# A third norm taken row by row inside the last feed-forward round, state-space tables made in that round, and three waits on weight rests moved

## What is computed

```python
# first block (end)
h = rms_norm(x, norm_ffn)
ff = square(relu(h @ w_ff1))          # 1024 -> 4096
x = x + ff @ w_ff2                    # 4096 -> 1024
x = rms_norm(x, norm_final)           # the "third norm"
# second block
u, h, c_gate, b_gate, gate_a, gate_b = split(x @ w_in_2 + b_in_2)
y_a = s5_ssm(u, ...)                  # 32 groups of 16 channels, 64 complex states each
#   dt = exp(log_dt); lb = exp(lambda * dt); powers of lb; (lb - 1) / lambda * b
y_a = gelu(y_a) * sigmoid(gelu(y_a) @ glu_w + glu_b) @ w_ssm_out
y_b = (b_gate * causal_conv(c_gate * h)) @ w_conv_out
merged = sigmoid(gate_a) * y_a + sigmoid(gate_b) * y_b
x = layer_norm(ALPHA * x + merged @ w_o)
x = layer_norm(ALPHA * x + (silu(x @ w_gate) * (x @ w_up)) @ w_down)
```

## Time and profile before

| | |
|---|---|
| median of 3 runs | 2930.26 us (2927.21 to 2930.47) |
| the profiled execution | 2929.72 us, its span 2927.8 us |
| TensorE (PE) busy | 2784.1 us, 95% of the span |
| VectorE (DVE) busy | 1293.1 us, 44% |
| ScalarE (ACT) busy | 710.6 us, 24% |
| GpSimd (POOL) busy | 288.1 us, 10% |
| mean granted TensorE clock | 0.979 |
| chain that ended last | PE 86%, DVE 9%, ACT 2%, issue 2%, DMA 1% |
| a 1 MB feed-forward slab, issue to landing | 5.4 us |

### The profile page before, as it was taken

The page is one execution under the profiler, slowest core; times in us unless marked ns, Lnnn a source line. Parts: engine busy times, 40 slices in busy tenths (PEclk is TensorE's granted clock), DMA queues, the critical chain, the costliest instruction groups (busy, mean ns, idle before and its releaser), DMA issues.

```text
span 2927.8 us, 34813 instructions
## 1 busy us (share of the span) xinstructions
PE 2784.1 (95%) x14570; PEld 2163.6 (74%) x14570; DVE 1293.1 (44%) x1909; ACT 710.6 (24%) x1172; POOL 288.1 (10%) x160
## 2 busy tenths in 40 slices
PE   5999997996999999999998999999999999999998
PEld 2445446884468888888877888877897888888877
DVE  1465695774243333333338433434264333333325
ACT  4224335321131112221131222222222111121112
POOL 0000143420000000000001121115400000000000
PEclk9999998996999999999999999999999999999999
DMA  4002004203011111111112222234312111112101
GB/s 152 29 30 87 29 18 155 86 33 137 0 65 44 43 57 54 47 43 45 56 39 86 66 73 87 71 120 148 137 38 79 43 43 43 43 44 71 43 15 72
DMA packets 161698, 188.17 MB, mean 64 GB/s; under 512 B 13488, under 2 KB 119216, under 8 KB 160944
## 3 DMA queue, kind: packets, MB, share of 16 engines
q1 hardware_dynamic: 161584, 186.54, 19.7%
HBM read 160.10 MB, written 25.23 MB: 63 GB/s over the span
## 4 chain that ended last, share of the span: by engine, by line
PE 86%; DVE 9%; ACT 2%; issue 2%; DMA 1%; POOL 0%; DVEq 0%; SPq 0%; ACTq 0%
PE ps L1209 65%; PE ps L907 6%; PE ps L1175 4%; DVE sb L2183 2%; PE ps L972 2%; DVE sb L2185 2%; PE ps L879 1%; PE ps L1079 1%; PE ps L1371 1%; PE ps L1121 1%; DVE sb L2258 1%; PE ps L1117 1%; PE ps L1093 1%; DVE sb L2431 1%; PE ps L915 1%
## 5 line engine op out<-in xcount | busy, mean ns | idle before, releaser
L1209 PE MATMUL ps<-H_hi,v_hi 128*128 128x512 f32 x704 | 274.9, 391 | 8.7 <-DVE v_lo L2729 5.6
L1209 PE MATMUL ps<-H_lo,v_hi 128*128 128x512 f32 x704 | 274.6, 390 | 0.0
L1209 PE MATMUL ps<-H_hi,v_lo 128*128 128x512 f32 x704 | 274.4, 390 | 0.0
L1209 PE MATMUL ps<-F_hi,w_hi 128*128 128x512 f32 x512 | 200.0, 391 | 3.4 <-DVE F_lo L2350 3.4
L1209 PE MATMUL ps<-F_lo,w_hi 128*128 128x512 f32 x512 | 199.9, 390 | 0.0
L1209 PE MATMUL ps<-F_hi,w_lo 128*128 128x512 f32 x512 | 199.7, 390 | 0.0
L1209 PE MATMUL ps<-w_hi,ff_hi 128*128 128x512 f32 x512 | 199.2, 389 | 0.0
L1209 PE MATMUL ps<-w_lo,ff_hi 128*128 128x512 f32 x512 | 199.2, 389 | 0.0
L1209 PE MATMUL ps<-w_hi,ff_lo 128*128 128x512 f32 x512 | 199.2, 389 | 0.0
L2760 DVE TENSOR_TENSOR hg<-hg,ps 128x512 f32<-128x512 f32 x44 | 30.3, 688 | 357.2 <-PE ps L1209 357.2
L1209 PE MATMUL ps<-H_hi,tw_hi 128*128 128x512 f32 x448 | 176.5, 394 | 8.6 <-DVE sb L2668 8.6
(11 more groups left out here) (335 smaller groups left out, 5272.6 us busy)
## 6 DMA issues: line engine op xcount, KB each, us to landing
wraw<-in_w_ff SPq DMA_DIRECT2D x32, 1024.0 KB, 5.4
traw<-in_w_in SPq DMA_DIRECT2D x28, 512.0 KB, 4.4
sb<-in_w_in SPq DMA_DIRECT2D x6, 2048.0 KB, 7.9
vraw<-in_w_gate SPq DMA_DIRECT2D x22, 512.0 KB, 5.1
vraw<-in_w_up SPq DMA_DIRECT2D x22, 512.0 KB, 6.2
vraw<-in_w_down SPq DMA_DIRECT2D x11, 1024.0 KB, 4.8
sb<-in_x SPq DMA_DIRECT2D x4, 2048.0 KB, 10.2
sb<-c_rows SPq DMA_DIRECT2D x16, 512.0 KB, 4.9
```

The costliest lines, as they stand in the source:

```text
L1209: mm = nc.tensor.matmul(out_ap, stationary(a, k), moving(c, k), start=(k == 0 and n == 0), stop=(k == kts - 1 and n == 2))
```

## The change

The third norm is taken row by row. The second half of the last round's down product gets its own order of groups, `last_order`, with the transposes of row t-2 behind row t and the input product's rows behind them. The input product takes a bank per half row, and U is drained in 16 parts. The tables' code moves unchanged into two functions, one called in k = 1 of the last round, one behind row 2 of its first half. Their loads (and those of three small tables) move in front of the feed-forward's rounds. The buffers of the third norm's results change place. Three waits on rests: the output product asks for 15 rests for rows 0 to 3 and for 16 from row 4; the first output weights are split after ft = 5 instead of 6; slab 0 of the last round of the second feed-forward is split after q = 1 of the round before instead of after q = 3.

```diff
+def last_order():
+    order = []
+    for t in range(NT):
+        order += [("w", t)] + [("t", t - 2, h) for h in range(2) if t > 1]
+    for t in range(0, 4, 2):
+        order += [("u", 0, t), ("u", 0, t + 1)] + [("t", 6 + t // 2, h) for h in range(2)]
+    order += [("u", 0, t) for t in range(4, NT)] + [("u", 1, t) for t in range(NT)]
+    return {key: n for n, key in enumerate(order)}
...
 @block.sync
...
             sp.dma_start(gain, A["norm_final"].partition_broadcast(P)).then_inc(gain_in, 16)
+            sp.dma_start(s_lr, A["lam_re"]).then_inc(ssm_in, 16)
+            sp.dma_start(s_li, A["lam_im"]).then_inc(ssm_in, 16)
...
+            sp.dma_start(taps2, A["conv_taps_2"].rearrange("p (t k) -> p t k", k=3)).then_inc(b2_in, 16)
             rounds(sp, FF_ROUNDS, ff_loads)
...
+            wait_drained(sp, last_ff, 7)
             sp.dma_start(u_row, ...).then_inc(u_row_in, 16)
             for j in range(NT):
                 sp.wait_ge(norm_rows, 16 + j + 1)
-                sp.dma_start(x_rows[j], xn[:, j, :]).then_inc(x_out, 16)
+                sp.dma_start(x_rows[j], xl[j]).then_inc(x_out, 16)
+            sp.wait_ge(x_out, 16 * NT)
+            wait_full(sp, *last_rows("t", NT - 1, 1))
+            sp.dma_start(d_row, A["ssm_d"].partition_broadcast(P)).then_inc(d_row_in, 16)
...
 @block.tensor
...
             def ff_round(i, last):
...
+                        if last and h == 1 and t > 1:
+                            pe.wait_ge(norm_rows, 2 * NT + t - 1)
+                            turn_row(last_rows, xl[t - 2], t - 2)
             rounds(pe, FF_ROUNDS, ff_round)
-            rows_to_features(G_NORM3, xn)
...
+            pe.wait_ge(u_lo, 1)
+            for t in range(NT):
+                if t in (2, 4):
+                    j = NT - 3 + t // 2
+                    pe.wait_ge(norm_rows, 2 * NT + j + 1)
+                    turn_row(last_rows, xl[j], j)
+                rows_ready(last_rows, [t])
+                input_rows(0, t)
+            pe.wait_ge(u_lo, 2)
+            for t in range(NT):
+                input_rows(1, t)
...
-            pe.wait_ge(m_lo, 16)
             for c in range(2):
                 pe.wait_ge(wo_lo, c + 1)
                 for t in range(NT):
+                    if c == 0 and t % 4 == 0:
+                        pe.wait_ge(m_lo, 15 + t // 4)
...
 @block.scalar
...
             def ff_round(i, last):
...
                     if h == 0:
                         round_slab(3, i)
+                        if last:
+                            act.wait_ge(ssm_angle, 1)
+                            nc.scalar.activation(s_sin, s_th, ACT.Sin)
+                            nc.scalar.activation(s_half, s_th, ACT.Sin, scale=0.5).then_inc(ssm_sin, 1)
...
+            round_input_weights(0)
+            act.wait_ge(w_lo, 4 * FF_ROUNDS)
+            for t in range(NT):
+                wait_drained(act, last_ff, 8 + t)
+                wait_drained(act, *last_rows("w", t))
+                nc.scalar.activation(xl[t], X[:, t, :], ACT.Square, accum_out=ssum[:, t:t + 1]).then_inc(norm_sums, 1)
+                root(1, t)
+                if t > 1:
+                    round_row(last_rows, t - 2, Hs[0])
+            for t in (NT - 2, NT - 1):
+                round_row(last_rows, t, Hs[0])
+            round_input_weights(1)
...
-                if ft == 6:
+                if ft == 5:
                     round_wo(0)
...
+                    if isinstance(i, int) and i == F2_ROUNDS - 2 and q == 1:
+                        wait_full(act, start, 3)
+                        round_slab2(0, i + 1)
...
 @block.gpsimd
...
-                if ft == 6:
+                if ft == 5:
                     rest_wo(0)
...
 @block.vector
...
             def ff_round(i, last):
...
                     if k in (1, 4):
                         rest_slab(1 + k // 4, i)
+                    if last and k == 1:
+                        state_rates()
-                for h in range(2):
+                for h in range(1 if last else 2):
                     for t in range(NT):
...
+                        if last and t == 2:
+                            state_powers()
             rounds(dve, FF_ROUNDS, ff_round)
...
+            for t in range(NT):
+                b = wait_full(dve, *last_rows("w", t))
+                xs = X[:, t, 512:1024]
+                V.tensor_tensor(xs, xs, ps[:, b, :], ALU.add).then_inc(drained[b], 1)
+                if t > 0:
+                    last_scaled(t - 1)
+                dve.wait_ge(norm_sums, 2 * NT + t + 1)
+                V.tensor_scalar(rs_arg[:, t:t + 1], ssum[:, t:t + 1], 1.0 / D, EPS, ALU.mult, ALU.add).then_inc(root_ask, 1)
+                if t > 1:
+                    rest_row(last_rows, t - 2, Hs[0], xrest, 1)
+            last_scaled(NT - 1)
+            rest_row(last_rows, NT - 2, Hs[0], xrest, 1)
+            dve.wait_ge(norm_rows, 3 * NT)
+            dve.wait_ge(u_row_in, 16)
+            input_drain(0, 0)
+            input_drain(0, 1)
+            rest_row(last_rows, NT - 1, Hs[0], xrest, 1)
+            input_drain(0, 2)
+            input_drain(0, 3)
             dve.wait_ge(x_out, 16 * NT)
...
             angles(0)
+            for t in range(4, NT):
+                input_drain(0, t)
             step_weights(0)
-            for j in range(NT):
-                b = wait_full(dve, G_U, j)
-                V.tensor_tensor(U[:, j, :], ps[:, b, :], u_row, add).then_inc(drained[b], 1)
+            for t in range(NT):
+                input_drain(1, t)
...
+                    if isinstance(i, int) and i == F2_ROUNDS - 2 and q == 1:
+                        rest_slab2(0, i + 1)
...
                 if isinstance(i, int) and i == F2_ROUNDS - 2:
-                    for q in range(2):
-                        rest_slab2(q, i + 1)
+                    rest_slab2(1, i + 1)
```

More of the change, by code:

```diff
@@ L331, in build @@
         xn = area(AT_WORK + 8192, NT, D)
+        xl = [area((AT_WORK + 8192, AT_WORK + 16384)[t // 4] + D * (t % 4), D) for t in range(NT)]
         BZ = area(AT_WORK, WT, SEQ)
-        U = area(AT_WORK + 4096, NT, W2)
+        U = area(AT_X + 4096, NT, W2)
         YA = area(AT_WORK + 4096, WT, SEQ)
-        U2 = area(AT_WORK + 4096, 4, D)
         M = area(AT_WORK + 8192, KT, SEQ)
@@ L1878, in f2_round @@
                 if not last:
-                    for q in range(2 if isinstance(i, int) and i == F2_ROUNDS - 2 else 3):
+                    for q in (1,) if isinstance(i, int) and i == F2_ROUNDS - 2 else range(3):
                         wait_full(act, start, (3, 7, 23)[q], **at)
@@ L2366, in rest_slab, with tt2, ts2, exp_to @@
                                 ).then_inc(w_lo, 1)
+            mul, add, sub = ALU.mult, ALU.add, ALU.subtract
+            def tt2(out, a, b, op):
+                then(V.tensor_tensor(out, a, b, op))
+            def ts2(out, a, x, op0, y=None, op1=None):
+                if op1 is None:
+                    then(V.tensor_scalar(out, a, x, None, op0))
+                else:
+                    then(V.tensor_scalar(out, a, x, y, op0, op1))
+            def exp_to(out, x):
+                ts2(s_k, x, 1.0 / float(np.log(2.0)), mul, -1e6, ALU.max)
+                ts2(s_k, s_k, ROUNDER, add)
+                ts2(s_k, s_k, ROUNDER, sub)
+                then(V.scalar_tensor_tensor(s_r, s_k, -LN2_HI, x, mul, add))
+                then(V.scalar_tensor_tensor(s_r, s_k, -LN2_LO, s_r, mul, add))
+                ts2(s_r, s_r, -1.0, ALU.max, 1.0, ALU.min)
+                ts2(s_e, s_r, 1.0 / 5040, mul, 1.0 / 720, add)
+                for c in (1.0 / 120, 1.0 / 24, 1.0 / 6, 0.5, 1.0, 1.0):
+                    tt2(s_e, s_e, s_r, mul)
+                    ts2(s_e, s_e, c, add)
+                ts2(s_k, s_k, -127.0, ALU.max, 128.0, ALU.min)
+                ts2(s_k, s_k, 127.0, add, 8388608.0, mul)
+                then(V.tensor_copy(s_t1.bitcast(mybir.dt.int32), s_k))
+                tt2(out, s_e, s_t1, mul)
@@ new lines, in reduce_angle, with power_rows @@
+            def reduce_angle(out, x, k, clamp_out=None):
+                ts2(k, x, 1.0 / TWO_PI, mul, ROUNDER, add)
+                ts2(k, k, ROUNDER, sub)
+                then(V.scalar_tensor_tensor(out, k, -TWO_PI_HI, x, mul, add))
+                then(V.scalar_tensor_tensor(out, k, -TWO_PI_LO, out, mul, add))
+                return V.tensor_scalar(out, out, PI_IN, -PI_IN, ALU.min, ALU.max)
+            def power_rows(first, count, by):
+                lo, hi = slice(1, 1 + count), slice(first, first + count)
+                xr = pw_re[:, by, :].unsqueeze(1).broadcast_to([P, count, 16])
+                xi = pw_im[:, by, :].unsqueeze(1).broadcast_to([P, count, 16])
+                n = count * 16
+                t0, t1 = (early[q][:, 0:n].rearrange("p (a b) -> p a b", b=16) for q in range(2))
+                tt2(t0, pw_re[:, lo, :], xr, mul)
+                tt2(t1, pw_im[:, lo, :], xi, mul)
+                tt2(pw_re[:, hi, :], t0, t1, sub)
```

(12 more changed lines are left out.)

246 lines of the change are left out of this document (88 added, 158 removed).

## The result

Six runs of the changed kernel have a median of **2902.82 us** (2900.0 to 2905.1), six of the kernel before 2928.99 us (2927.21 to 2934.91). The ratio is 0.9908, 95% interval 0.9895 to 0.9921: 26 us faster. The prediction was 2902, range 2895 to 2911.

What follows compares the result with a forecast made beforehand. TensorE, busy 95% of the span, bounds the kernel, so only its stops and restarts can be won. Gains 14.9 - 0.5 + 5.9 + 7.4 = 27.7 us, from 2929.7, gave 2902 us, range 2895 to 2911.

Steps and rivals of the forecast that it cites:

- first tile earlier: Third norm's tail: first state-space tile starts at 1590.8 instead of 1603.8, 13.0 us, less 0.5 for a clock fall.
- no restart there: At the first state-space tile: without the 8.6-us stop, no slow-clock restart behind it, 1.9 us gained.
- merge stage: Output product: waiting for 15 rests and splitting weights earlier removes a 4.2-us stop and 1.7 us of restart; bounds 3.3 and 5.9.
- last round: Second feed-forward's last round: the earlier split of slab 0 removes a 5.6-us stop and 1.8 us of restart.
- The rates: State rates at k=1 of the last round: 16.3 us of VectorE, hidden by k=6, costed at nothing.
- The powers: State powers behind row 2 of the last round's first half: 15.3 us without POOL beside them, bounds 15.0 and 19.5.
- the table load: Row 0 of the third norm: the load for the root, behind the new sine, lies beside the path.
- The bank was free: First state-space tile: its bank is free at 1579 to 1589, with 2 to 11 us to spare.
- The pace: Third norm, rows 1 to 5: VectorE paces at 4.87 us a row against TensorE's 3.6; bounds 3.6 and 5.6.
- Rows slower: Third norm: powers keep 19.5 us or the table load costs 4 us, and rows take 5.3; 2908 us, 17%.
- A seam that doesn't close: Merge stage or last weight rest: a wait behind eats one small move, 5.9 or 7.4 us back; 2908 us, 10%.
- Slower by the clock: Third norm's rows and input product: the clock falls at 1516 and stays at half, net 30 us slower; 2960 us, 3%.

Runs made afterwards that it cites:

- POOL in the powers: Changed kernel with the cast of the first input weights right behind the sines, so GpSimd's 4.6-us pass falls into VectorE's powers: 2907.41 us.
- the variants: Changed kernel with part of the powers moved into VectorE's idle time (2897.27 us), with VectorE's rests one row cycle later (2902.3 us), or with both (2895.71, again 2893.5 us).
- the kernels with single edits: Changed kernel with only the output product's wait back to 16 rests: 2910.77 us; with only the first output weights' split back behind the seventh tile: 2904.3 us.
- the kernel with only the split back: Changed kernel with the split of the first output weights back behind the seventh tile, the wait staying at 15 rests: 2904.3 us.

## Why the prediction was right, step by step

The time, 2902, lies 0.8 us from the median of the first six runs. With the nine later ones the changed kernel's median is 2904.7, because ten of 15 fell on the upper level; the profiled execution, against which the sum was made, was at 2900.7. The sum's terms, against what the traces give (all positions of after are 1.5 us early from the start):

| term | predicted | before to after | same falls of the clock on both sides |
|---|---|---|---|
| first tile earlier | 13.0 - 0.5 | 12.8 | 12.8 |
| no restart there | 1.9 | 1.9 | 1.9 |
| merge stage | 4.2 + 1.7 | 3.7 + 1.7 | 4.3 + 1.7 |
| last round | 5.6 + 1.8 | 6.1 | 7.4 |
| sum | 27.7 | 26.2 | 28.1 |
| not forecast: clock behind the GLU's stop (at 1965 before) | 0 | 1.3 | 0.7 |
| not forecast: clock behind the 3.07-us stop | 0 | in the 6.1 | -1.3 |
| not forecast: earlier by the last round, in the main the clock near the start | 0 | 1.5 | 1.5 |
| all | 27.7 | 29.0 | 29.0 |

The last column takes each term from profiles in which the same stops lowered the clock. G to Z is 391.0 where it fell at the GLU's stop and no restart stood at G (POOL in the powers), so 1.9 of the 3.2 us are the restart and 1.3 the GLU's fall. The profiles with that fall have a Z to W 0.6 shorter (87.1 against 87.7), which gives back 0.6 of the 1.3.

**The norm's seam.** The rates (1457.7 to 1473.6) were hidden, as said: they shift the rest behind k = 4 by 4.7 us from the span's start (6.2 with the 1.5), and by the eighth cast VectorE waits 3.9 us for ScalarE again. The powers took 15.2 us (15.3 said). Row 0 was scaled by 1517.98 where, less 1.5, 1518.1 was said; row 5 by 1540.74 (1540.6); the first tile started at 1589.54 (1589.3). One step inside was wrong without harm: the table load of 1.28 us was said to lie beside the path, and lies on it. ScalarE squares row 0, loads, and only then takes the root VectorE waits for:

```profile
1513.91 1.28 ACT L1499 ACT_TABLE_LOAD   x1
```

VectorE's reciprocal at 1515.51 stands behind it by 0.83 us. It was paid by the 4.87 us taken for row 0, a full cycle with two rests (1.29 us) and a wait of 0.74 in it that row 0 does not have; in their place stood the waits of 1.30 us for the square and 0.83 for the root. Two errors of some 2 us met, and that row 0 came out to 0.1 us is luck. The bank was free as said: the step weights ended at 1580.4, inside the 1579 to 1589 less 1.5.

**The pace.** From row 2 on rows came every 4.85 us with 0.74 of waiting, as taken from the earlier trace rows, and the variants show both the pace setter (VectorE) and the reserve (0.84 us a row). Row 2 took 5.4, which is the 0.5 charged for the clock. TensorE's short stops were 0.55, 1.0 and 1.0 us ahead of rows 3 to 5, where some 1.3 ahead of each row was said.

**The merge stage.** The 15th rest was said to be ready 1.0 us ahead of TensorE; it was 1.07. The split's 1 us and the count's 4.2 are what the kernels with single edits show.

**The last round.** The mechanism and the price hold (7.4 when it alone is undone). The two profiles give 6.1 because of another stop of this stage. Its first timeline row is of the kernel before, the second of the one after:

```profile
2202.96 0.47 PE L1209 MATMUL ps<-H_hi,v_hi 128*128 128x512 f32 x1 [3.07 <-DVE H_lo L2350]
```

```profile
2180.09 0.77 PE L1228 MATMUL ps<-H_hi,v_hi 128*128 128x512 f32 x1 [3.07 <-DVE H_lo L2373]
```

The same stop of 3.07 us, 16 us into the stage; the matmul behind it took 0.47 us at full clock before and 0.77 at half clock after. That cost after 1.3 us. (In the kernel with only the split back the clock did not fall there either, and its F to E is 733.2, the shortest of all.) The other way round at the GLU's stop of 2.9 us, the row of before first:

```profile
1966.00:1968.00 2.00, 2.00 (x4) 0.92 (x3) 0.00 (x0) 0.00 (x0) 0.00 (x0) 0.50 1.00 412
```

```profile
1950.00:1952.00 2.00, 2.00 (x6) 0.83 (x5) 0.00 (x0) 0.00 (x0) 0.00 (x0) 1.00 1.02 418
```

The edits touch neither stop, and near 60 us the same program was seen both with and without a fall; that these two were chance as well is argued, since no second profile of the kernel before was taken. **What the prediction lacked** is this: it took the 1.7 to 1.9 us behind a stop as fixed, and compared sums of one execution to tenths. The terms themselves come to 28.1 against 27.7; that the total came out near 2902 is partly luck, in which falls of the clock the profiled runs had (+0.7, -1.3, +1.5) and on which level the runs fell.

**The rivals.** Rows slower: its table load came true, its price did not. A seam that doesn't close: not seen; the 13th rest was pushed towards the 14th's time as feared (they start at 2057.6 and 2060.2, with 1.28 us of POOL idle between them), and the 15th was not late. Slower by the clock: the clock did fall at the predicted place, and was back 4 us later in a stretch of stop and go with transposes. The Trainium skill's rule that transposes do not count as busy (TensorE: Matmul & The Clock Gate) would have kept it low by that rival; this trace does not bear that out for transposes mixed with matmuls. But the prediction's ground against this rival, "in every restart it was back within 4 us", was a wrong reading. The trace of the kernel before has a stretch in which the transposes run alone, four at a time with stops between, and there the clock stayed low:

```profile
692.97 1.11 PE L879 MATMUL ps<-sb 128*128 128x128 f32 x4 [17.18 <-DVE sb L2341]
695.03 1.11 PE L879 MATMUL ps<-sb 128*128 128x128 f32 x4 [0.94 <-DVE sb L2341]
```

```profile
692.00:709.00 17.00, 8.92 (x32) 5.72 (x32) 14.78 (x23) 4.59 (x8) 0.00 (x0) 0.50 0.70 250
```

It came back only at 713, behind 3.6 us of matmuls. That stretch agrees with the Trainium skill's rule; whether the transposes or the stops kept the clock low there, no run separates. So the rival had a precedent in this very kernel, and its 3% rested on less than the prediction thought. In the new seam twelve matmuls of 512 columns stand between the transposes of two rows, and the stops are 1.0 us at most behind the first.

## What to carry to other kernels

A norm can be taken row by row under the matmuls that produce its rows; then the engine that does the rows' elementwise work sets the pace, and whatever it does besides (here the tables' powers) should be cut to fit its idle times, with the other engine's passes over SBUF kept out of them. Where a consumer waits for n partial results, ask how many its first step reads: one count changed was worth more than the move of the work behind it. And before a difference of 5 us is read as an edit's, compare the stages' distances and the clock behind each stop, since the same program ran 5 us apart, 3.3 of it by one fall of the clock at 60 us.

## What the runs showed of the hardware

**Whether the clock falls behind a short stop, and what the fall costs, varies.** Over 14 profiles of this family: behind the stop of 0.76 us near 58 us it fell in 6, behind the GLU's 2.9 us in 4, behind the 1.9 to 2.5 us ahead of the merge stage in 1, behind the 3.07 us of the second feed-forward's start in 12, behind the third norm's 3.15 us in all 8 that had it; behind 4.2, 5.6 and 7.3 us always; behind 1.04 us (one profile) not. For the first of these the same program shows both (not in two profiles of the changed kernel, but in the third); at the other stops different kernels are compared. A fall cost 0.5 us where there was slack, 1.3 to 1.9 where the clock was soon back, and 2.8 and 3.3 where it stayed low for some 6.8 us (2070 to 2078 and 60 to 68 above). The Trainium skill (TensorE: Matmul & The Clock Gate, Part 1) says of a kernel's start that the number of slow matmuls varies from run to run; what is seen here is the same kind of variation at stops further in.

**VectorE held by GpSimd, one instruction for all of a pass.** Besides the 4.50-us copy above, a sum of two SBUF operands of 128x512 in the merge stage took 4.68 us from 2052.2 in the changed kernel (0.69 elsewhere), beside POOL's 4.61 us from 2051.7. It had slack there: with the wait for 16, Z to W is 92.0 us with the split at either place, though with the split undone the operation was held only 2.9 us. In the input product one of 128x512 took 3.98 us from 1558.9, beside POOL's 4.62 from 1557.7.

**A table load costs its 1.28 us and no more.** It starts 0.02 us behind the activation before it, and the root starts 1.30 us after the load does. The Trainium skill (ScalarE: Activation LUTs, "What ACT_TABLE_LOAD costs") adds a drain of as much again to each switch; the measurement here does not agree, as no row leaves room for it.
